# Feed-forward layer as one stage, normed key/value and query inputs made inside their stages, other orders in the output norm and in sample attention

## The reference

```python
def rms_norm(x, g):
    y = xf * lax.rsqrt(jnp.mean(xf * xf, axis=-1, keepdims=True) + EPS)
    return (y * g.astype(jnp.float32)).astype(x.dtype)

def conv_ffn(h, conv_prev, g_norm, w_up, w_gate, conv_w, conv_b, w_down):
    xn = rms_norm(h, g_norm)
    u = xn @ w_up
    gp = xn @ w_gate
    gc = conv_b + sum over j of conv_w[j] * (gp shifted by 2 - j tokens, after conv_prev)
    return h + (jax.nn.silu(gc) * u) @ w_down, (the last two tokens of gp)

# end of the time mixing: per head of 64, then gain, bias, bonus, gate and the product with w_o
y = ((y - mu) * lax.rsqrt(var + GN_EPS)) * lnx_w + lnx_b
out = ((y + bonus) * g) @ w_o

kv = rms_norm(h, kv_norm) @ w_kv            # key/value side, after layer 0
q = rms_norm(rms_norm(h, ln_mix[1]) @ nsa_wq, nsa_qnorm) * HEAD_DIM ** -0.5
# each sample: softmax over 255 compressed blocks, over the 16 best of 65 blocks, over a window of 512
```

## Time and profile before

| | |
|---|---|
| median of three runs | 3016.11 us |
| the profiled execution | 3014.09 us, span 3012.3 us |
| TensorE busy | 2562.3 us (85%), 25248 matmuls, mean granted clock 0.915 |
| VectorE, ScalarE, GpSimd busy | 1412.0, 831.1, 788.3 us |
| up, gate and down matmuls of both layers (L334) | 6336, 847.0 us |
| moved by transfers | 276.22 MB, mean 92 GB/s |

### The profile page before, as it was taken

How to read it: one execution, slowest core, us unless ns; L and a number is a source line. 1 busy time by engine, 2 the same in 40 slices (tenths; PEclk the granted TensorE clock), 3 DMA queues, 4 the chain that set the end, 5 groups by cost and what they waited for, 6 DMA issues and landing times. The chain is left out here.

```text
span 3012.3 us, 61936 instructions
## 1 busy us (share of the span) xinstructions
PE 2562.3 (85%) x25248; PEld 2024.8 (67%) x25248; DVE 1412.0 (47%) x2862; ACT 831.1 (28%) x1881; POOL 788.3 (26%) x480
## 2 busy tenths in 40 slices
PE   5998999838699979597998878878888876999798
PEld 3776999616699979444443655545555554999798
DVE  6208565341477710102334246657667743577600
ACT  2215334130222221001111135545545521122210
POOL 0001000100476633000000049921111100667541
PEclk8999999769799989797999879989989988999999
DMA  2121001101222221316883100035444521222231
GB/s 93 56 65 39 4 4 32 51 14 56 65 84 84 77 99 57 138 56 243 306 294 112 45 15 2 1 135 182 164 161 162 178 70 44 84 82 80 70 106 60
DMA packets 107842, 276.22 MB, mean 92 GB/s; under 512 B 13353, under 2 KB 14250, under 8 KB 105450
## 3 DMA queue, kind: packets, MB, share of 16 engines
q1 hardware_dynamic: 107626, 273.18, 27.0%
HBM read 264.42 MB, written 16.97 MB: 93 GB/s over the span
## 5 line engine op out<-in xcount | busy, mean ns | idle before, releaser
L334 PE MATMUL ps<-parts 128*128 128x288 f32 x6336 | 847.0, 296 | 87.6 <-POOL parts L303 87.6
L334 PEld LDWEIGHTS ps<-parts 128*128 128x128 f32 x6336 | 846.1, 189 | 88.3 <-issue 88.3
L303 POOL TENSOR_TENSOR parts<-kept,parts 128x1024 fp32r<-128x1024 f32 (+1 forms) x120 | 314.8, 2625 | 180.2 <-ACT parts L298 173.3
L308 POOL TENSOR_TENSOR parts<-kept 128x1024 fp32r<-128x1024 f32 x88 | 179.3, 2037 | 461.5 <-DMA kept<-in_wall 304.3
L1660 PE MATMUL ps<-mix,kept 128*128 128x512 f32 (+1 forms) x544 | 227.8, 579 | 0.0
L1342 DVE TENSOR_TENSOR kept<-kept,ps 128x576 f32 x32 | 24.2, 756 | 421.4 <-PE ps L334 294.3
L2080 POOL TENSOR_SCALAR mix<-kept 128x896 f32<-128x896 f32 x16 | 40.4, 2524 | 573.1 <-SPq L2070 573.1
L1660 PEld LDWEIGHTS ps<-mix,kept 128*128 128x128 f32 x544 | 101.3, 194 | 120.0 <-issue 120.0
L2543 POOL TENSOR_TENSOR mix<-mix 128x512 f32<-128x512 f32 x64 | 66.7, 1042 | 394.7 <-DVE mix L2246 368.0
L2094 POOL TENSOR_SCALAR mix<-mix 128x128 f32<-128x128 f32 (+3 forms) x128 | 136.3, 1084 | 23.6 <-DVE mix L2055 23.6
L1453 DVE TENSOR_SCALAR kept<-kept 128x512 f32<-128x512 f32 x44 | 72.2, 1641 | 125.4 <-ACT kept L1430 125.4
(11 more groups left out here) (426 smaller groups left out, 4829.0 us busy)
## 6 DMA issues: line engine op xcount, KB each, us to landing
mix<-in_cmp_pool SPq DMA_DIRECT2D x256, 256.0 KB, 4.9
mix<-in_slc_pool SPq DMA_DIRECT2D x192, 256.0 KB, 3.4
kept<-in_wall SPq DMA_DIRECT2D x88, 512.0 KB, 3.6
mix<-in_wall SPq DMA_DIRECT2D x48, 512.0 KB, 3.6
kept<-in_wdown SPq DMA_DIRECT2D x32, 704.0 KB, 4.0
kept<-in_slc_pool SPq DMA_DIRECT2D x64, 256.0 KB, 3.4
out_s_win<-in_state_win SPq DMA_DIRECT2D x1, 8064.0 KB
mix<-in_wkv SPq DMA_DIRECT2D x1, 6144.0 KB, 17.2
```

The costliest lines, as they stand in the source:

```text
L303: return e.tensor_tensor(low.bitcast(F32R), whole, high, ALU.subtract)
L308: e.tensor_tensor(high.bitcast(F32R), whole, c.c("one").to_broadcast([P, whole.shape[1]]), ALU.mult).then_inc(*steps.step())
L334: mm = pe.matmul(out, l[:, f, :].bitcast(F32R), m[:, first + f, a:b].bitcast(F32R), start=first + f == 0 and k == 0, stop=last and f == n ...
```

## The change

1. *Output norm.* Four centred buffers; squares, final tiles and roots have buffers of their own; VectorE runs centre f, scale f-2, gate f-3, ScalarE square f, root f-1, gain f-2.
2. *Feed-forward.* Norm, up/gate and down are one stage. SP loads weight blocks and GpSimd splits them from the stage's start. TensorE's first two blocks (up, gate) go tile by tile: for each f both blocks, as soon as the low part of f is there. The down loads begin when GpSimd has split the last gate block; GpSimd makes both parts of the first two halves itself, the other 14 as before; the down products wait for what they need only, with four PSUM tiles in turn. The loop over down halves is written out. The conv state's output lies in the place of `rs`.
3. *Key/value side and query.* The norm moves into `kv_side`; the weights come as eight transfers ahead of everything on SP; the first group waits tile by tile for normed input and weights. `compress` gets its own root buffer, so that `rs` stays; `query` makes its normed input from h, `rs` and the other gain; the second `rms_norm` is gone.
4. *Sample attention.* TensorE does `spreads` before `means`; VectorE does correction and inverse root at the end of the step; ScalarE does the squares before the root; the inverse root has two buffers in place of three.

```diff
-    two = lambda k: [c.v(MEM["A"] + (k + j) * NT, NT) for j in range(2)]
-    mid, sq, root, root2 = two(0), two(2), two(4), two(6)
+    some = lambda at, n: [c.v(at + j * NT, NT) for j in range(n)]
+    mid, sq, fin = some(MEM["A"], 4), some(MEM["A"] + 4 * NT, 2), some(MEM["A"] + 6 * NT, 2)
+    root, root2 = some(MEM["K"], 2), some(MEM["K"] + 2 * NT, 2)
...
-                if f >= 2:
-                    v.wait_ge(*A.at(seg, f"gain{f - 2}"))
-                v.scalar_tensor_tensor(out=halves(mid[f % 2]), in0=banks(ps("mean", f)), scalar=-1.0 / HD,
+                if f >= 4:
+                    v.wait_ge(*A.at(seg, f"gain{f - 4}"))
+                v.scalar_tensor_tensor(out=halves(mid[f % 4]), in0=banks(ps("mean", f)), scalar=-1.0 / HD,
                                        in1=halves(y[:, f]), op0=ALU.mult, op1=ALU.add).then_inc(*V.step(f"mid{f}"))
...
-            for f in range(FT + 2):
+            for f in range(FT + 3):
                 if f < FT:
                     centre(f)
-                if 0 <= f - 1 < FT:
-                    scaled(f - 1)
                 if 0 <= f - 2 < FT:
-                    gated(f - 2)
+                    scaled(f - 2)
+                if 0 <= f - 3 < FT:
+                    gated(f - 3)
...
                     if f >= 2:
-                        act.wait_ge(*V.at(seg, f"out{f - 2}"))
-                    act.activation(sq[f % 2], mid[f % 2], ACT.Square).then_inc(*A.step(f"sq{f}"))
...
+                        act.wait_ge(*T.at(seg, f"var{f - 2}"))
+                    act.activation(sq[f % 2], mid[f % 4], ACT.Square).then_inc(*A.step(f"sq{f}"))
+                if 0 <= f - 1 < FT:
+                    m = f - 1
+                    r, e = root[m % 2], root2[m % 2]
+                    act.wait_ge(*T.at(seg, f"var{m}"))
+                    if m >= 2:
+                        act.wait_ge(*V.at(seg, f"unit{m - 2}"))
+                    act.activation(halves(r), banks(ps("var", m)), ACT.Ln, bias=c.c("gn_eps")).then_inc(*A.step())
...
-                    act.activation(e, r, ACT.Square).then_inc(*A.step(f"root{f}"))
-                if 0 <= f - 1 < FT:
-                    m = f - 1
+                    act.activation(e, r, ACT.Square).then_inc(*A.step(f"root{m}"))
+                if 0 <= f - 2 < FT:
+                    m = f - 2
                     act.wait_ge(*V.at(seg, f"unit{m}"))
-                    act.activation(sq[m % 2], mid[m % 2], ACT.Identity, bias=c.col("lnx_b", m),
+                    if m >= 2:
+                        act.wait_ge(*V.at(seg, f"out{m - 2}"))
+                    act.activation(fin[m % 2], mid[m % 4], ACT.Identity, bias=c.col("lnx_b", m),
...
+            sp.wait_ge(*G.at(seg, "split3", last))
+            for u, (m, k) in enumerate(UNITS):
+                if u == 1:
+                    sp.wait_ge(*V.at(seg, "parted0", last))
+                if u >= 2:
+                    sp.wait_ge(*G.at(down, f"rest{u - 2}"))
+                sp.dma_start(raw[u % 2], d["wdown"][m + layer * FT, :, k * HALF_FF * P:(k + 1) * HALF_FF * P]).then_inc(
+                    down_got[u % 2].sem, 16)
...
+            T.begin(seg, 0)
+            for j in range(2):
+                pe.wait_ge(*G.at(seg, f"split{j}"))
+            for f in range(FT):
+                pe.wait_ge(*V.at(norm, f"low{f}"))
+                for j in range(2):
+                    for o, a, b in BANKS:
+                        for k, (l, m) in enumerate(((0, 0), (0, 1), (1, 0))):
+                            mm = pe.matmul(c.ps[j][:, o:o + b - a], w[j][l][:, f].bitcast(F32R),
+                                           x[m][:, f, a:b].bitcast(F32R), start=f == 0 and k == 0,
+                                           stop=f == FT - 1 and k == 2)
+                    if f == FT - 1:
+                        mm.then_inc(*T.step(f"mm{j}"))
+            for j in range(2, 4):
+                pe.wait_ge(*G.at(seg, f"split{j}"))
+                for o, a, b in BANKS:
+                    mm = product(pe, c.ps[j][:, o:o + b - a], w[j % 2], x, 0, True, a, b)
...
+            T.begin(down)
+            for u, (m, k) in enumerate(UNITS):
+                pe.wait_ge(*G.at(down, f"rest{u}"))
+                if k == 0:
+                    if m >= 4:
+                        pe.wait_ge(*V.at(down, f"added{m - 4}"))
+                    else:
+                        pe.wait_ge(*(A.at(seg, f"gate{m // 2}", last) if m % 2 else V.at(seg, f"prod{m // 2}", last)))
+                else:
+                    pe.wait_ge(*V.at(seg, "parted1", last))
+                for o, a, b in BANKS:
+                    mm = product(pe, c.ps[m % 4][:, o:o + b - a], dw[u % 4], F, k * HALF_FF, k == 1, a, b)
+                mm.then_inc(*T.step(f"mm{u}"))
+            T.end()
...
+            G.begin(down)
+            for u in range(len(UNITS)):
+                if u < 2:
+                    g.wait_ge(down_got[u].sem, 16)
+                    g.wait_ge(*T.at(seg, f"mm{2 + u}", last))
+                    split(c, g, G, raw[u], *map(flat, dw[u])).then_inc(*G.step(f"rest{u}"))
+                else:
+                    g.wait_ge(*A.at(down, f"rounded{u}"))
+                    rest(g, raw[u % 2], *map(flat, dw[u % 4])).then_inc(*G.step(f"rest{u}"))
...
+            for u in range(2, len(UNITS)):
+                act.wait_ge(down_got[u % 2].sem, 16 * (u // 2 + 1))
+                if u < 4:
+                    act.wait_ge(*T.at(seg, "mm3", last))
+                else:
+                    act.wait_ge(*T.at(down, f"mm{u - 4}"))
+                rounded(act, raw[u % 2], flat(dw[u % 4][0])).then_inc(*A.step(f"rounded{u}"))
...
+            def low(f):
+                v.wait_ge(*A.at(norm, f"rounded{f}"))
+                rest(v, unit[f % 3], x[0][:, f], x[1][:, f]).then_inc(*V.step(f"low{f}"))
+
+            for f in range(FT):
+                if f >= 3:
+                    v.wait_ge(*V.at(norm, f"low{f - 3}"))
+                v.scalar_tensor_tensor(out=unit[f % 3], in0=h[:, f], scalar=c.col(f"ln_ffn{layer}", f), in1=rs,
+                                       op0=ALU.mult, op1=ALU.mult).then_inc(*V.step(f"normed{f}"))
+                if f:
+                    low(f - 1)
+            low(FT - 1)
...
-            sp.dma_start(c.v(KVM["w"], FT * 1536), d["wkv"]).then_inc(*got.more())
+            for f in range(FT):
+                sp.dma_start(c.v(KVM["w"] + f * 1536, 1536), d["wkv"][:, f * 1536:(f + 1) * 1536]).then_inc(*got[f].more())
...
-            pe.wait_ge(*got.all())
+            for f in pairs:
+                pe.wait_ge(*V.at("kv", f"pair{f}"))
+                for a, b in ((0, SEQ), (SEQ, NT)):
+                    mm = pe.matmul(c.ps[3][:, a:b], c.c("mean"), x[:, f, a:b], start=f == pairs[0], stop=f == pairs[-1])
+            mm.then_inc(*T.step("squares"))
...
+                        if n == 0:
+                            pe.wait_ge(*V.at("kv", f"normed{f}"))
+                            pe.wait_ge(*got[f].all())
...
-    bk, bv, rr = c.v(CMPX["bk"], 2 * NCS), c.v(CMPX["bv"], 2 * NCS), c.v(MEM["rs"], 2 * NCS)
+    bk, bv, rr = c.v(CMPX["bk"], 2 * NCS), c.v(CMPX["bv"], 2 * NCS), c.v(CMP["root"], 2 * NCS)
...
+            for f in range(FT):
+                v.scalar_tensor_tensor(out=x[:, f], in0=h[:, f], scalar=c.col("ln_mix1", f), in1=rs, op0=ALU.mult,
+                                       op1=ALU.mult).then_inc(*V.step(f"normed{f}"))
...
-                if 0 <= t + 1 < last:
-                    n = t + 1
-                    m, r = mean[n % 2], inv[n % 3]
-                    v.wait_ge(*A.at(seg, f"rs{n}"))
-                    v.scalar_tensor_tensor(out=m, in0=meansq[:, 0:P], scalar=EPS, in1=u, op0=ALU.add,
-                                           op1=ALU.mult).then_inc(*V.step(f"u{n}"))
-                    v.wait_ge(*V.own())
-                    v.scalar_tensor_tensor(out=r, in0=m, scalar=3.0, in1=r, op0=ALU.subtract,
-                                           op1=ALU.mult).then_inc(*V.step(f"r{n}"))
                 vector_side(v, i, k)
...
+                if 0 <= t + 1 < last:
+                    n = t + 1
...
             for t, i, k in ticks():
+                if 0 <= t - 1 < last:
+                    spreads(pe, t - 1)
                 if 0 <= t + 1 < last:
                     means(pe, t + 1)
-                if 0 <= t - 1 < last:
-                    spreads(pe, t - 1)
                 if 0 <= t < last:
                     scores(pe, t)
...
-            rms_norm(c, "norm_kv", MEM["h"], MEM["x"], "kv_norm")
             kv_side(c)
             compress(c)
-            rms_norm(c, "norm_mix1", MEM["h"], MEM["x"], "ln_mix1")
             query(c)
```

272 lines of the change are left out of this document (151 added, 121 removed).

## The result

The changed kernel takes 2818.98 us, median of 4 runs (2814.16 to 2822.31), against 3016.2 us for the kernel before on the same chip: ratio 0.9345, 95% interval 0.9328 to 0.9361. The forecast was 2854 us, 35 us too long, and the measured time lies inside its range of 2816 to 2892, 3 us above the lower end. The profiled execution took 2821.6 us (span 2819.8).

| stage | before | after | gain | forecast |
|---|---|---|---|---|
| output norm, to the first product behind it | 85.6 | 44.7 | 40.8 | 38.7 |
| feed-forward, layer 0 (norm included) | 477.3 | 455.1 | 22.2 | 24.4 |
| feed-forward, layer 1 (norm included) | 484.0 | 461.2 | 22.8 | 24.4 |
| key/value side, to the compression | 170.0 | 145.1 | 24.9 | 22.7 |
| query, with its norm | 117.6 | 97.2 | 20.4 | 19.8 |

What follows compares the result with a forecast made beforehand. TensorE bounds the big product stages; at the seams little or nothing runs on it. Gains 38.7 + 48.8 + 22.7 + 19.8 + 32 = 162 off 3014.1 us, with 2.0 added, give 2854 us; range 2816 to 2892.

Steps and rivals of the forecast that it cites:

- Output norm: Output norm: more buffers open the ring of VectorE and ScalarE waits, leaving VectorE the bound; gain 38.7 us.
- Norm to up: Each layer's norm to first up matmul: weight loads and splits start with the norm; gain 9.4 us a layer.
- The pause: After the first two up/gate blocks: TensorE waits 4.3 us while GpSimd splits block 2 into the same buffers.
- I take 1.5: Norm to up, each layer: clock cost of TensorE's restart, 1.5 us taken off the gain.
- Gate to down: Each layer's last gate to first down matmul: earlier down loads and GpSimd splits; gain 15 us a layer, clock included.
- Key/value and query: Stage starts: early loads in eighths and tile-by-tile waits gain 22.7 us; dropping the query's second norm gains 19.8.
- Sample attention: Sample attention: new order opens the ring of waits; 14 plain steps, 10 compressed softmax, 8 net others; gain 32 us.
- (c): Sample attention: TensorE becomes the bound everywhere and the clock stays up; gain 62 us, time 2824 us; chance 0.11.
- (a): GpSimd beside VectorE holds up norm and last unit: feed-forward seams 16 a layer, key/value 17; 2877 us; chance 0.14.
- (b): Sample attention: new order only moves the wait to the means, gives nothing; 2886 us; chance 0.12.
- (d): Down stage: without the pause before it, TensorE's clock falls to its lower level; +276, 3130 us; chance 0.02.
- (e): Stages: overlap does not come about; only output norm, query and the order act; 2925 us; chance 0.03.

Runs made afterwards that it cites:

- the short splits: Changed kernel with ScalarE rounding each layer's first two weight blocks, GpSimd taking only their rests: 2813.01 us; together with block 0 first, 2806.16 us.
- block 0 first: Changed kernel with the first 96 up and gate products reordered, block 0 taking each norm tile as it comes, block 1 filling between: 2807.11 us, ratio 0.9305.
- the kernel that shares no tiles: Changed kernel with the means sent to the same output columns as their group's scores, spread's table turned to match: 2826.89 us, ratio 0.9376.
- all-old: Changed kernel with all sample attention orders as before and three buffers for the root, all else as changed: 2888.95 us, ratio 0.958.

## Why the prediction was right, and where it was not

**Output norm** (38.7, measured 40.8): right in its reason. VectorE's six instructions still take 750 to 760 ns, and the waits that the ring made are gone.

**Norm to up** (9.4 a layer, measured 6.6 and 7.3): right in its reason, with one part mis-sized. The start came 20.9 us after the norm's start in layer 0 and 19.85 in layer 1, forecast 19.2, within the bounds; in layer 0 the mean products took 7.26 us for layer 1's 6.23, at a clock of 0.62 for 0.73. The pause was 3.64 us in both layers against 4.3. The clock's part, "I take 1.5", was too small: the up and gate products were busy 284.95 and 284.89 us where they had been 281.65 and 281.27, 3.3 and 3.6 more, with a clock of 0.87 in the 15.85 us from the first of them. In layer 0 the refined root was ready 18.4 us after the start. The three small instructions of the refinement take 6.40 us beside GpSimd and 1.98 alone, 4.4 us more; with the short splits, 2.5 us of that came back (first up product after 17.3 us in place of 19.85, block 0 first in both). The Trainium skill (SBUF — State Buffer, "SBUF: two separate sides") has a GpSimd instruction that came first hold the shared ports to its end against a VectorE instruction with two SBUF inputs, or one in a two-port mode. The trace agrees: the scaling (2.03 us for 0.46) and the last product (2.77 for 0.76) end 0.3 and 0.6 us after the GpSimd instruction that was running when they started. The scaling reads a single tensor; which mode it ran in no run shows.

**Gate to down** (15 a layer, measured 15.6): right; TensorE restarts 2.35 us after its last gate product, since GpSimd's split of the first half, 6.15 us long (1017.87 to 1024.02), begins 3.9 us before that. The 0.65 more here and the 2 to 3 us less at the norm give about the two layers' 22.2 and 22.8.

**Key/value and query** (22.7 and 19.8; 24.9 and 20.4): right. First products at 13.9 and 3.3 us, forecast 14.7 and 3.6. The Trainium skill's 1 MiB rule (DMA: Bandwidth & Descriptors, "Rules for kernel authors") spoke against 768 KB pieces; here the eight landed 10.0 us after issue at the median, the one of 6144 KB 17.9 after it, and the stage was 5.6 us shorter with the eight.

**Sample attention** (32, measured 65.5): the step that failed is "TensorE's own 4.88 - 0.55 = 4.33 us bound a plain step. About 25 of 72 steps are plain", with "I take 8 us net from these, since VectorE's sum stays and the clock's dips remain". Cut into steps as above, the two profiles show what came in its place. The 23 plain steps gave 12.9 us, near the 14 booked, but not as booked: 18 of them went from 4.88 to 4.13 us, 0.76 each for 0.55, since TensorE's own part is 4.13 and not 4.33 even with nothing shared (with shared tiles it is less, but the 0.31 us of wait fills the step); four became up to 0.4 us longer. The 7 steps with the compressed softmax gave 19.0, where 10 were booked for 8 (the first sample's softmax comes ahead of these steps): the wait fell by 0.8 us each (28.3 to 21.7 in all 8), and the time at the lower clock in them from 34 to 14 us. The other 41 gave 32.5, where 8 were booked, and not by waits: TensorE's time without a matmul in them went from 38.3 to 41.2 us, its busy time from 214.7 to 179.2. Nor did VectorE's sum stay: it fell by 27.6 us, as shown above; what that alone is worth in time was not tested.

The term counted waits and nothing else, and as that it was not far off: the kernel that shares no tiles lost 32 us of waits against all-old. What it missed was booked nowhere: 18 us of clock, since fewer waits mean less time at the lower level, 15 of own work that a 128-row product between the 64-row groups had cost, and 8.7 from shared tiles, at most. With the 32 these sum to 74; before itself stood 8.7 us under all-old, which leaves the 65.5. Before and all-old have the same order in this stage; most of those 8.7 us are the clock (0.89 and 0.87), and why it differs stays open.

The rivals: (c) named 62 us and 2824, nearest in number, but not in its mechanism, for TensorE is not the bound everywhere; 87.6 us without a matmul remain, and the prediction doesn't say how the 62 is made up. The disturbance of (a) is there, 4.4 us a layer, but the forecast had booked 3.9 of it (766.1 for 762.2), and the layers gave 22.2 and 22.8, not 16. (b), (d) and (e) did not come: the clock stayed at 0.98 and 0.99 through the long products.

That the time lies in the range at all owes something to luck: one term was off by 33.5 us, and without the 4.1 us that the unchanged stages ran longer in the profiled execution, the median would stand at the range's lower edge.

## What to carry to other kernels

Price a wait twice in a stage that runs near TensorE's bound: once as idle time, once as matmuls at the lower clock behind it, here about one to one (6.9 and 7.3 us in the stage, 7.4 and 6.0 in the steps concerned). Ask also what an instruction that is moved will run beside: VectorE's inverse root lasted 1083 ns beside GpSimd's masks and 292 alone. When an order is changed on several engines, don't value the parts alone: here VectorE's and ScalarE's new order was worth +22 us with TensorE's and -42 without it. Less work on the busiest engine is no gain while a ring of waits sets the step: 34 us less came with 16 us more time in one order, and 22 less with 8.7 less in another.

## What the runs showed of the hardware

Small matmuls on different tiles of the array ran at the same time, and on the same tile one after the other: 1.56 and 1.94 us for the same 40 matmul records. The record even has the first four scores start at 2030.95, ahead of the last twelve means at 2031.03 that stand before them in the program. And a 128-row product between two 64-row groups cost something by itself: own work 336 with it, 321 without, both with nothing shared (an estimate, since the clock differed too), and 4.33 against 4.13 us in a plain step. The Trainium skill has both (TensorEngine Tiling (Array Packing), "Key Properties": different tiles work in parallel, a change of tiling mode drains the engine). The 1.56 us agree with the first, and the 0.2 us a plain step fit the second, though no run shows the drain itself. Weighing that page against the order of the groups would have pointed to the smaller own work ahead of time, though not to its size or the time.

VectorE's instructions lasted longer beside GpSimd's, those that read one tensor too: the scaling of the refinement 2.03 us for 0.46, that of the compressed softmax 1.22 for 0.35.
